# Conformer and neighbourhood-attention encoder block: V's later weight pieces issued ahead of the first bias rows, and in the last pair the probabilities stored ahead of the next weight piece, with the reloads of the gated values behind their reads

## The reference

```
h = rmsnorm(x); [a, glu, zA, q, k, v, zB, gates] = h @ w_in
ya = (silu(layernorm(conv31(a * sigmoid(glu)))) * silu(zA)) @ w_pw_a
yb = (neighbourhood_attention(q, k, v, bias) * silu(zB)) @ w_o_b
y = rmsnorm(x + (sigmoid(gA) * ya + sigmoid(gB) * yb) @ w_out)
```

## Time and profile before

| | us |
|---|---|
| median of 3 runs | 1808.8 |
| the profiled execution, its own time | 1807.6 |
| its span | 1805.7 |
| TensorE busy | 1744.9 |
| VectorE busy | 1174.6 |
| ScalarE busy | 468.1 |
| GpSimd busy | 206.6 |

### The profile page before, as it was taken

The page is one execution under the profiler, slowest core; times in us unless marked ns, Lnnn a source line. Parts: engine busy times, 40 slices in busy tenths (PEclk is TensorE's granted clock), DMA queues, the critical chain, the costliest instruction groups (busy, mean ns, idle before and its releaser), DMA issues.

```text
span 1805.7 us, 24607 instructions
## 1 busy us (share of the span) xinstructions
PE 1744.9 (97%) x8652; PEld 1411.0 (78%) x8652; DVE 1174.6 (65%) x1765; ACT 468.1 (26%) x925; POOL 206.6 (11%) x250
## 2 busy tenths in 40 slices
PE   7959999999999999999999999999987999999998
PEld 6848887878877887888887788788776777887886
DVE  4417645898588589669768948957974667435332
ACT  4411123132122213212222312222224334103122
POOL 1110011011011102101101101110200055000001
PEclk9979999999999999999999999999998999999999
DMA  7250335636535544634543553563556656533223
GB/s 282 66 86 35 88 75 133 180 102 166 143 81 143 134 112 127 166 94 117 168 131 88 152 131 93 141 166 89 146 181 222 221 171 197 187 118 107 90 82 129
DMA packets 293893, 240.97 MB, mean 133 GB/s; under 512 B 117222, under 2 KB 248310, under 8 KB 293658
## 3 DMA queue, kind: packets, MB, share of 16 engines
q1 hardware_dynamic: 241482, 145.69, 29.7%
q10 hardware_dynamic: 48432, 79.97, 13.1%
q0 software_dynamic: 3872, 13.75, 2.9%
HBM read 155.10 MB, written 84.23 MB: 133 GB/s over the span
## 4 chain that ended last, share of the span: by engine, by line
PE 87%; DVE 5%; DMA 4%; issue 2%; ACT 1%; POOL 1%; SPq 0%; ACTq 0%; DVEq 0%
PE pg L1411 66%; PE pg L1429 14%; PE pO L1524 3%; PE pS L1507 3%; DVE work L1307 1%; DMA qk<-gb_d 1%; DMA work<-p_d 1%; DVE work L1313 1%; DVE ws L1039 1%; DMA raw<-in_w_in 1%; POOL rel_d L618 0%; DVE xs L1047 0%; DVE work L1292 0%; DMA rel_d<-work 0%; DVE work L1324 0%
## 5 line engine op out<-in xcount | busy, mean ns | idle before, releaser
L1411 PE MATMUL pg<-xs,ws 128*128 128x512 f32 x5688 | 1326.9, 392 | 5.2 <-DVE work L1324 4.0
L1411 PEld LDWEIGHTS pg<-xs,ws 128*128 128x128 f32 x5688 | 1062.0, 188 | 247.4 <-issue 20.8
L1123 DVE SCALAR_TENSOR_TENSOR work<-work 128x1551 f32<-128x1551 f32 x240 | 438.4, 1827 | 4.4
L1429 PE MATMUL pg<-ws,xs 128*128 128x512 f32 x1008 | 238.8, 393 | 3.1 <-DVE ws L1039 1.9
L1429 PEld LDWEIGHTS pg<-ws,xs 128*128 128x128 f32 x1008 | 189.5, 189 | 44.2 <-DVE ws L1039 4.4
L632 POOL TENSOR_TENSOR work<-work 128x384 f32<-128x384 bf16 (+1 forms) x72 | 62.5, 867 | 991.5 <-DVE small L1195 981.2
L1195 DVE CUSTOM_DVE_ANT_0 work<-pS,work 128x384 f32<-128x384 f32 (+1 forms) x192 | 88.4, 510 | 120.1 <-PE pS L1507 119.2
L1039 DVE TENSOR_TENSOR ws<-raw,ws 128x1024 fp32r<-128x1024 f32 x89 | 109.9, 1235 | 68.8 <-ACT ws L683 68.8
L900 ACT ACTIVATE work<-work,small 128x384 f32<-128x384 f32 (+1 forms) x192 | 109.2, 570 | 158.1 <-DVE small L1195 158.1
L683 ACT ACTIVATE ws<-raw 128x1024 fp32r<-128x1024 f32 x89 | 93.5, 1053 | 123.5 <-PE pg L1411 83.3
L1207 DVE STREAM_TRANSPOSE work<-work 128x384 f32<-128x384 f32 (+1 forms) x192 | 102.6, 534 | 6.6
(11 more groups left out here) (98 smaller groups left out, 909.2 us busy)
## 6 DMA issues: line engine op xcount, KB each, us to landing
raw<-in_w_in SPq DMA_DIRECT2D x70, 512.0 KB, 4.2
p_d<-work SPq DMA_DIRECT2D x256, 96.0 KB, 2.1
work<-p_d ACTq DMA_DIRECT2D x64, 384.0 KB, 3.8
work<-v_d SPq DMA_DIRECT2D x128, 96.0 KB, 2.7
p_d<-work SPq DMA_DIRECT2D x128, 64.0 KB, 1.9
work<-p_d ACTq DMA_DIRECT2D x32, 256.0 KB, 2.7
v_d<-work ACTq DMA_DIRECT2D x24, 256.0 KB, 2.0
za_d<-work ACTq DMA_DIRECT2D x24, 256.0 KB, 2.1
```

The costliest lines, as they stand in the source:

```text
L1123: nc.vector.scalar_tensor_tensor(cv[:, 0:CLEN], u[:, k:k + CLEN], cur[:, k:k + 1], cv[:, 0:CLEN], ALU.mult, ALU.add).then_inc(tap_ok, 1)
L1411: last = nc.tensor.matmul(pg[b][:], wt(s, wpart)[:, k * P:(k + 1) * P], xs[:, k, xpart, chunk(n)], start=(k == 0 and wpart == 1), stop=(k ...
L1429: last = nc.tensor.matmul(pg[b][:], xs[:, k, xpart, t * P:(t + 1) * P], wt(s0 + k // 2, wpart)[:, chunk(k % 2)], start=(k == 0 and xpart = ...
```

## The change

Three things in SyncE's program and one in ScalarE's. In the first stage the four weight pieces 8 to 11 are issued before the first bias rows of head 0. In the last pair the piece `S_YB` + 1 stands behind all stores of probabilities. The seven reloads wait in addition until all reads of probabilities have landed (`p_in`). ScalarE takes A's first group before it splits V2's third piece.

```diff
--- before.py
+++ after.py
@@ -467,14 +467,14 @@
                         sp.dma_start(vb[BAND * r:BAND * r + BAND, :, j, :], src).then_inc(v_in, 16)
 
 
-            sp.wait_ge(x_lo, 3 * KT)
-            sp.wait_ge(rel_out, 16 * QB)
-            load_rel(0, 0, (0,))
             for s in range(S_V2 + 2, S_Q):
                 piece_s(s, w_rows(w0, C_V * P + CH, s - S_V2))
             for s, c in ((S_Q, C_Q), (S_K, C_K)):
                 piece_s(s, w_tile(w0, c * P))
 
+            sp.wait_ge(x_lo, 3 * KT)
+            sp.wait_ge(rel_out, 16 * QB)
+            load_rel(0, 0, (0,))
             sp.wait_ge(w_used, 6)
             load_rel(0, 0, (1,))
             for n in range(3):
@@ -507,8 +507,8 @@
                     if n < len(ahead):
                         s = s_of(i) + n + 2
                         piece(s, w_tile(w0, i * P + ahead[n] * P), 8 * i + (s - 1))
-                    elif last and n < 6:
-                        piece_y(S_YB + n - 4)
+                    elif last and n == 4:
+                        piece_y(S_YB)
                     if n < BLOCKS // 2:
                         store_probs(i, 2 * n)
                         store_probs(i, 2 * n + 1)
@@ -528,11 +528,14 @@
                 sp.dma_start(xre[:, e % 4, :], tok_rows(x_prompt, x_sample, t)[:, c * CH:(c + 1) * CH]).then_inc(
                     xr_in[e % 4], 16)
 
+            piece_y(S_YB + 1)
             sp.wait_ge(tb_out, 16 * (PAIRS - 1))
 
             def load_tb(k):
                 sp.dma_start(home(k), tb_d[k]).then_inc(tbs_in, 16)
 
+            for n in range(2):
+                sp.wait_ge(p_in[n], 96 * PAIRS)
             sp.wait_ge(qk_done, BLK * PAIRS)
             load_tb(3)
             sp.wait_ge(t_ok, BLK * PAIRS)
@@ -777,11 +780,13 @@
 
             split_s(S_GLU)
             take_v(NT - 1)
-            for s in range(S_V2, S_V2 + 3):
+            for s in range(S_V2, S_V2 + 2):
                 split_s(s)
             act.wait_ge(pads_ok, 3)
             for n in range(NCH):
                 take_a(*grs(G_A + n)[:2], n)
+                if n == 0:
+                    split_s(S_V2 + 2)
             split_s(S_V2 + 3)
             for n in range(NCH):
                 b, done, _ = grs(G_GLU + n)
```

## The result

The changed kernel takes 1780.2 us (median of 4, 1778.8 to 1781.4) against 1808.8 us before (1807.8 to 1808.8): ratio 0.9843, 95% interval 0.9826 to 0.9860, or 28.6 us faster. The forecast was 1777 in a range of 1771 to 1788. The profiled execution took 1781.4 us with a span of 1779.5, so it is one of the longer ones; against the one profiled before it gained 26.2 us of the 31.5 that the sum gave.

A forecast was written before the change was run, and what follows sets the result against it. The prediction took TensorE, busy 1744.9 of 1805.7 us, as the bound; 20.3 (pause) + 1.8 (clock) + 9.4 (last pair) = 31.5 us off 1807.6 gave 1776.1, plus 1.2 to the median: 1777, range 1771 to 1788.

The forecast's parts named there:

- The pause of 20.3 us: First stage, TensorE's wait from 100.66: put down to SyncE's queue order; 20.3 us go, with 1.8 us of clock.
- The third piece's landing: First stage, V2's third weight piece beside the table's writes: lands at about 100.5, at the latest 104.8 if slowed threefold.
- rival A: First stage: the weight piece lands only after the table's writes, at 115.8; part 1 is 9.1 us, time 1790; chance 0.08.
- Nobody misses the bias rows: First stage: head 0's bias rows go out later, at about 109; costed at 0, with some 100 us of slack.
- The reloads are what is late next: End of last pair: the seven reloads' last landing, at 1366.5, sets ScalarE's refill of chunk 0, 9.4 us earlier.
- a sign of being wrong: End of last pair: probabilities read in over 6 us would show the prediction wrong.
- The wait for the first gate: Behind the last pair: a TensorE wait of about 5 us for the first gate, named as a sign of being right.
- the last pair's part: End of last pair, stores moved ahead and reloads held back: worth 9.4 us, bounds 2.4 and 15.1.
- D: End of last pair: the wait before the reloads costs more than it brings, time passes 1812.4; chance 0.02.
- B: End of last pair: reloads run at 0.258 MB/us; part 2 is 2.5 us, time 1784; chance 0.14, including part-way.
- C: End of last pair: reloads early enough, TensorE sets the pace; part 2 is 15.1 us, time 1771.6; chance 0.11, including part.

## Why the prediction was right, and where it was too large

**The pause of 20.3 us and its cause: right.** The releaser named was the last link of a queue order on SyncE, and moving the pieces took it away. The sum gave 22.1 us; TensorE's lead at V2's first tokens is 21.8, and the first stage alone measures 20.8.

**The third piece's landing: inside its bound, the delay too small and of another kind.** The step took the delay as an addition, 4.1 us on top of 4.2, landing at 100.5. It landed at 103.1, 10.8 us after its issue, against 12.6 for the threefold slowing that was the bound. Nor was it slowed evenly: by the rows of the queues it stood still until 98, behind the table's writes, as rival A says. Part of the good end is luck. The prediction has the writes run on until 111.6, but GpSimd issued ten from 88.3 to 93.6, the last of which landed at 103.0, and the other six only from 103.45. The kernel before shows the same break (six from 103.01), which the prediction didn't look at. The piece came in with the ten and before the six; behind all sixteen it would have been late, by rival A's own sum. The bound of 104.8 was kept by some 1.6 us, so nothing came of it. The run with SyncE's order alone shows what the same landing costs where the first evacuation waits for it: 4.3 us of pause.

**Nobody misses the bias rows: right,** shown by holding them 20 us longer.

**The reloads are what is late next: right, the term mis-sized.** The last landing was put at 15.9 us after the first issue (the terms themselves, 14.8 and 1.4, give 16.2); it took 17.6. The sum counted the seven reloads and a gate store, but not the weight piece `S_YB` + 2, issued at 1335.03 right behind them, 0.52 MB, which at 0.39 MB/us is 1.3 us: all 6.3 MB at that rate and 1.4 us fixed make 17.5. Block 11's read took 6.2 us, just over the 6 that were named as a sign of being wrong, and not the 4.4 worked out; TensorE waited 1.58 us for it and not 0.6. So SyncE began 1.0 us later against TensorE's progress than worked out. The refill gained 27.1 - 20.4 = 6.7 us instead of 9.4. Some of it came back: ScalarE no longer waited for TensorE between the refills (1.0 us), and the first gate's read was 0.9 us shorter. At the fourth gate 7.5 us were left. By median the last pair's part is 8.1 us (1788.3 less 1780.2) or 9.5 (alone).

**The wait for the first gate: right.** About 5 us were named, 4.3 were there. I had not priced what follows it. TensorE's clock, by the granted clock in the stretches' rows (third column from the right), falls:

```profile
1366.00:1368.00 2.00, 0.00 (x0) 0.00 (x0) 0.00 (x0) 0.00 (x0) 0.30 (x1) 0.99 1.06 424
1368.00:1370.00 2.00, 0.80 (x2) 0.70 (x3) 1.54 (x2) 0.00 (x0) 0.00 (x0) 0.50 1.02 409
1370.00:1372.00 2.00, 2.00 (x6) 1.51 (x6) 1.24 (x3) 0.00 (x0) 0.00 (x0) 0.50 1.02 391
```

TensorE's lead over the kernel before shrinks from 29.0 to 26.4 us in the matmuls at 1.2 GHz that follow, and is 27.9 again at the fourth gate, whose read both kernels wait for: of 2.6 us for the clock, 1.5 would have been waited anyway. That read, issued at 1370.73, took 16.9 us beside the reads of c_d.

**What the sum left out:** 1.4 us lost over the pairs and 1.7 us behind the fourth gate, in this one execution. The first stage alone kept its lead until the last values (22.1 us at V2's first tokens, 21.7 there), and the kernels with the table later and without the stores' move arrive there 0.9 and 1.7 us before the changed one, though nothing of the pairs differs; so I take the 1.4 us for variation between executions. Of the 1.7 us the larger part is a longer stretch at half clock around the column sums of the squares (24 small matmuls in 4.81 instead of 3.55 us). It is there in the first stage's kernel too, whose last pair is that of before. Why the clock stays down longer in some executions is open; no run here was made to settle it.

**The rivals.** A's price did not occur, though what it describes did for part of the writes, nor did D. B's rate did not occur, only a last landing 1.7 us later than the forecast's. C would have needed the reloads before the means, and ScalarE's wait of 6.68 us says that it didn't. On the transfer rate, the Trainium skill ("DMA: Bandwidth & Descriptors", Specifications) gives about 358 GB/s as a core's limit at its memory, which it works out as half of the 716 GB/s that two cores share. Here one core runs, and the rows above show 424 and 409 GB/s, so that figure doesn't bind in this case. The forecast's rate was not what went wrong, the bytes counted were.

## What to carry to other kernels

When a wait names an engine that finished long ago, walk the queue that fed it: here one in-order queue held weights behind a wait for a table and the rows read from it, and GpSimd, which took these rows, stood 98.3 us for the next ones in the kernel before. When a bulk reload follows a latency-critical read, hold it until the read has landed, then count every transfer behind it up to the wait that ends last, also those issued half a microsecond later. And put what needs no wait into the gap before the critical read: two reloads or three gate reads there brought the ratio from 0.9843 to 0.9819 (each time with intervals that still overlap a little), all the moves together (the gate reads then behind the reloads, the convolution's store later) to 0.9788, clear of it.

## What the runs showed that I had not expected

Ten writes of 69 KB made 512 KB reads on another queue take 10.8 us instead of 3.6, while the average rate there was no more than 129 GB/s:

```profile
88.00:98.00 10.00, 10.00 (x49) 7.89 (x49) 2.82 (x3) 3.32 (x4) 5.95 (x10) 1.00 0.95 129
```

The engines' share is 0.95 at that rate: it is time and not bytes that these writes take. They gather rows of 48 numbers, 192 bytes each, out of a wider table. By the rows of the queues they moved 0.32 MB in 87.7% of 5.7 us, which is 0.064 MB for each us of all engines, where the weights had 0.92 MB in 47.6% of 5 us, 0.39 MB: an estimated factor of six. That the short rows are the reason is not shown, since no run wrote the table in another form. And two edits that each shorten the same wait by another way (stores earlier, traffic held back) were worth 5.0 and 8.0 us alone and 8.1 together.
